# Attention steps in another order, the first unit chunk by chunk, and three sums moved in a hybrid decoder layer

## What is computed

```
x += 1/2 * SwiGLU_1(RMSNorm(x))                 # 1024 -> 2816 -> 1024
h  = RMSNorm(x);  p = h @ W_in
     gated linear attention: 4 heads, chunks of 64, a gate of rank 16
     dilated attention: 8 heads of 64, rotary on the first 16 of each head's dims
x += W_out @ concat(gla_out, attn_out)
x += 1/2 * SwiGLU_2(RMSNorm(x))
out = RMSNorm_final(x)
```

## Time and profile before

| | us |
|---|---|
| median of 3 runs (985.09 to 986.87) | 985.33 |
| the profiled execution's own time | 985.22 |
| its span in the trace | 983.4 |
| PE busy | 965.2 (98%) |
| DVE busy | 486.5 (49%) |
| ACT busy | 347.5 (35%) |
| POOL busy | 50.6 (5%) |

### The profile page before, as it was taken

One profiled execution on the slowest core, in us unless ns is written; L12 is line 12 of the kernel. 1 busy time (PEld: TensorE's weight loads), 2 busy tenths in 40 slices (PEclk: granted clock), 3 DMA queues, 4 the chain that ended last, 5 costly groups with the idle time before them and its releaser, 6 DMA issues.

```text
span 983.4 us, 11835 instructions
## 1 busy us (share of the span) xinstructions
PE 965.2 (98%) x4554; PEld 786.2 (80%) x4554; DVE 486.5 (49%) x616; ACT 347.5 (35%) x453; POOL 50.6 (5%) x35
## 2 busy tenths in 40 slices
PE   8999999999999999999989899999999999999997
PEld 6888888888888886888867678788888888888885
DVE  6854532244444456634386659644453234444325
ACT  7323221122232336331656764533322123322313
POOL 0850000000000000000021000000000000000000
PEclk9999999999999999999999999999999999999999
DMA  8232222323211233222121103223212232223212
GB/s 316 86 129 85 75 97 96 117 86 112 102 69 65 96 112 122 86 94 86 43 76 54 44 1 129 86 91 123 85 64 97 96 129 86 85 91 143 86 43 85
DMA packets 16305, 92.63 MB, mean 94 GB/s; under 512 B 1936, under 2 KB 2320, under 8 KB 8080
## 3 DMA queue, kind: packets, MB, share of 16 engines
q1 hardware_dynamic: 15984, 91.89, 26.4%
q10 hardware_dynamic: 288, 0.28, 0.1%
HBM read 90.07 MB, written 2.10 MB: 94 GB/s over the span
## 4 chain that ended last, share of the span: by engine, by line
PE 92%; DVE 3%; ACT 2%; issue 2%; DMA 1%; POOL 0%; SPq 0%; DVEq 0%; ACTq 0%; POOLq 0%
PE bank L1156 29%; PE bank L1157 28%; PE bank L1158 28%; PE bank L1467 1%; PE bank L1451 1%; PE bank L1437 1%; ACT w_hi L432 1%; DMA x<-in_xT 1%; DVE gt L963 0%; PE bank L1229 0%; PE bank L1359 0%; PE bank L1231 0%; PE bank L1236 0%; PE bank L1181 0%; PE bank L1410 0%
## 5 line engine op out<-in xcount | busy, mean ns | idle before, releaser
L1156 PE MATMUL bank<-h_hi,w_hi 128*128 128x512 f32 x824 | 323.8, 393 | 0.0
L1158 PE MATMUL bank<-h_hi,w_lo 128*128 128x512 f32 x824 | 320.7, 389 | 0.0
L1157 PE MATMUL bank<-h_lo,w_hi 128*128 128x512 f32 x824 | 320.7, 389 | 0.0
L432 ACT ACTIVATE w_hi<-raw 128x2048 fp32r<-128x2048 f32 (+2 forms) x88 | 156.6, 1779 | 338.2 <-PE bank L1158 336.7
L711 DVE TENSOR_TENSOR w_lo<-raw,w_hi 128x2048 fp32r<-128x2048 f32 (+2 forms) x88 | 187.0, 2125 | 85.2 <-ACT w_hi L432 85.0
L1156 PEld LDWEIGHTS bank<-h_hi,w_hi 128*128 128x128 f32 x824 | 154.7, 188 | 34.7 <-issue 2.1
L1157 PEld LDWEIGHTS bank<-h_lo,w_hi 128*128 128x128 f32 x824 | 154.7, 188 | 32.4 <-issue 1.0
L1158 PEld LDWEIGHTS bank<-h_hi,w_lo 128*128 128x128 f32 x824 | 154.7, 188 | 32.3
L757 DVE TENSOR_TENSOR prod<-bank,rstd 128x512 f32<-128x512 f32 x44 | 30.4, 690 | 183.6 <-PE bank L1158 183.6
L1156 PE MATMUL bank<-g_hi,w_hi 128*128 128x512 f32 x272 | 105.8, 389 | 0.0
L1157 PE MATMUL bank<-g_lo,w_hi 128*128 128x512 f32 x272 | 105.8, 389 | 0.0
(11 more groups left out here) (218 smaller groups left out, 858.8 us busy)
## 6 DMA issues: line engine op xcount, KB each, us to landing
raw<-in_up SPq DMA_DIRECT2D x43, 1024.0 KB, 4.8
raw<-in_w_proj SPq DMA_DIRECT2D x8, 1024.0 KB, 4.8
raw<-in_down1a SPq DMA_DIRECT2D x8, 768.0 KB, 4.3
raw<-in_down2a SPq DMA_DIRECT2D x8, 768.0 KB, 4.4
raw<-in_down1b SPq DMA_DIRECT2D x8, 640.0 KB, 3.8
raw<-in_down2b SPq DMA_DIRECT2D x5, 1024.0 KB, 4.8
raw<-in_w_v SPq DMA_DIRECT2D x4, 1024.0 KB, 4.8
raw<-in_w_o SPq DMA_DIRECT2D x4, 1024.0 KB, 4.8
```

The costliest lines, as they stand in the source:

```text
L432: nc.scalar.activation(w_hi[u % 2][:, 0:size], raw[u % 2][:, 0:size], ACT.Copy).then_inc(w_round, 1)
L1156: nc.tensor.matmul(out, a_hi, b_hi, start=first, stop=False)
L1157: nc.tensor.matmul(out, a_hi, b_lo, start=False, stop=False)
L1158: return nc.tensor.matmul(out, a_lo, b_hi, start=False, stop=last)
```

## The change

It has five parts.

1. **Start.** The first unit's weights go over ACT's DMA queue in four chunks, both tiles' columns together; SP loads `x` alone. PE makes both tiles of the unit chunk by chunk. ACT rounds unit 1 before it squares `x`.
2. **Channel sums.** In `second_unit` the channel sums stand behind tile 3, no longer before it; in the second FFN they stand behind the second tile of the first unit (`w == 1`).
3. **Gate weights.** Their scaling stands in the first FFN, before its first down phase.
4. **Attention.** Even steps divide both heads on DVE, odd steps both on ACT (from step 11: one each). DVE issues the rotation behind the scaling, `rotated` behind the concatenation; unit splits and head work move to other steps.
5. **The last split** of that loop, of unit U+14, is made in four quarters in steps 10 to 13 (ACT) and 11 to 14 (DVE).

```diff
@@ SP, phase
-                    for j, (lo, hi) in enumerate(FIRST_COLS):
-                        sp.dma_start(raw[0][:, lo:hi], source(0)[:, lo:hi]).then_inc(w_first[j], 16)
-                        sp.dma_start(x[:, j, :], xT_in[j]).then_inc(x_in[j], 16)
-                    for m in range(2, KC):
+                    for m in range(KC):
                         sp.dma_start(x[:, m, :], xT_in[m]).then_inc(x_in[m], 16)
-                    sp.dma_start(raw[0][:, D:UP_W], source(0)[:, D:UP_W]).then_inc(w_in[0], 16)
@@ ACT, start
+        FIRST_CHUNKS = ((0, 1), (1, 3), (3, 5), (5, KC))
+            for j, (_, hi) in enumerate(FIRST_CHUNKS):
+                landed = w_first[j] if hi < KC else w_in[0]
+                act.dma_start(first_part(raw[0][:], j), first_part(up1[0], j)).then_inc(landed, 16)
+                if j == 0:
+                    act.dma_start(gains[:].rearrange("p n a -> p (n a)"), gains_in).then_inc(gains_in_sem, 16)
             for m in range(KC):
...
+                for j, (lo, hi) in enumerate(FIRST_CHUNKS):
+                    if m == lo:
+                        act.wait_ge(w_first[j] if hi < KC else w_in[0], 16)
+                        nc.scalar.activation(first_part(w_hi[0][:], j), first_part(raw[0][:], j),
+                                             ACT.Copy).then_inc(first_round if hi < KC else w_round, 1)
-            for m in range(2):
-                square_first(m)
             split(1, 0, unit_size(1))
-            for m in range(2, KC):
+            for m in range(KC):
                 square_first(m)
@@ PE, first_unit, second_unit, up
+                                for w in range(2):
+                                    col = (w * KC + pos) * P
+                                    nc.tensor.matmul(ps[4 + w][:], w_hi[0][:, col:col + P], h_hi[:, pos, :],
+                                                     start=pos == 0, stop=False)
...
                         late_low(1, 0, 2, lambda: pe.wait_ge(w_round, 2), lambda: pe.wait_ge(w_split, 2))
+                        tile_of(1, 1, 3)
                         pe.wait_ge(const_landed, 32)
                         pe.wait_ge(first_sum, KC - 1)
                         channel_sums(0, 6, sumsq[:])
-                        tile_of(1, 1, 3)
...
-                            if first and w == 0 and layer:
+                            if first and w == 1 and layer:
@@ ACT, attention loop
+        SHARED_FROM = 11
+        def on_scalar(s, e):
+            return s % 2 == 1 if s < SHARED_FROM else e == 1
...
+            def round_quarter(u, q, tiles):
+                cols = slice(q * S, q * S + S)
...
-                if 1 <= k <= ATT_STEPS:
-                    scale_second(k - 1)
+                if 1 <= k <= ATT_STEPS and on_scalar(k - 1, 1):
+                    scale_scalar(k - 1)
                 if k >= 2:
                     move_probsT(k - 2)
-                if turn_of == 2 and n < 4:
+                if turn_of == 3 and n < 3:
                     split_next(U + 9 + n, 0, T + 19 + 2 * n)
+                if 10 <= k < 14:
+                    round_quarter(U + 14, k - 10, T + 25)
...
-                if turn_of == 3 and k >= 7:
-                    high_heads(k // 4 - 1)
+                if k in (9, 13, 15):
+                    high_heads((9, 13, 15).index(k))
@@ DVE, gate weights
+                    if layer == 0 and kind == "down" and a == 0:
+                        dve.wait_ge(ga_in, 16)
+                        nc.vector.tensor_tensor(w_gate[:], raw_ga[:],
...
@@ DVE, attention loop
-                if rotates:
-                    rotate(2 * n + turn_of // 2)
+                if k == 11:
+                    rotated(7)
                 if k:
                     scale_probs(k - 1)
                 if rotates:
-                    rotated(2 * n + turn_of // 2)
-                if turn_of == 2 and n < 4:
-                    split_next(U + 9 + n, 0)
+                    rotate(2 * n + turn_of // 2)
                 if k == 0:
                     gla_channel(3)
-                if 1 <= k <= 4:
-                    g = k - 1
+                if k in (1, 2, 4, 5):
+                    g = (1, 2, 4, 5).index(k)
                     low_concat(g, cat_lo[:, g, :], o_gla[g][:], cat_hi[:, g, :])
-                if turn_of == 3 and k >= 7:
-                    low_heads(k // 4 - 1)
-                if turn_of == 0 and k >= 12:
-                    add_heads(k // 4 - 2)
+                if rotates and k < 10:
+                    rotated(2 * n + turn_of // 2)
+                if turn_of == 3 and n < 3:
+                    split_next(U + 9 + n, 0)
+                if 11 <= k < 15:
+                    split_quarter(U + 14, k - 11)
+                if k in (9, 13, 15):
+                    low_heads((9, 13, 15).index(k))
+                if k in (14, 16):
+                    add_heads(k // 2 - 6)
```

More of the change, by code:

```diff
@@ L192, in layer_program @@
         const_landed = sem("const_landed")
-        w_first = [sem(f"w_first{j}") for j in range(2)]
+        w_first = [sem(f"w_first{j}") for j in range(3)]
         warm_zero = sem("warm_zero")
@@ L248, in layer_program @@
         ktail_out = sem("ktail_out")
-        probs_scaled = [sem(f"probs_scaled{e}") for e in range(2)]
+        dve_scaled = sem("dve_scaled")
+        act_scaled = sem("act_scaled")
         cat_round = sem("cat_round")
@@ L323, in head_tiles, with scaled_count @@
             return (o_hi[:, p, :], o_lo[:, p, :]) if p < 2 else (h_hi[:, 4 + p, :], h_lo[:, 4 + p, :])
+        def on_scalar(s, e):
+            return s % 2 == 1 if s < SHARED_FROM else e == 1
+        def scaled_count(s, e):
+            mine = on_scalar(s, e)
+            return sum(on_scalar(r, f) == mine for r in range(s + 1) for f in range(2) if (r, f) <= (s, e))
         def unit_size(u):
@@ L607, in exp_scores, with scale_scalar @@
                                          accum_out=den[:, q:q + 1]).then_inc(exp_done, 1)
[L609 to L612 removed]
+            def round_quarter(u, q, tiles):
+                cols = slice(q * S, q * S + S)
+                if q == 0:
+                    act.wait_ge(tile_done, tiles)
+                    act.wait_ge(w_in[u % 2], 16 * (u // 2 + 1))
+                nc.scalar.activation(w_hi[u % 2][:, cols], raw[u % 2][:, cols],
+                                     ACT.Copy).then_inc(quarter_round if q < 3 else w_round, 1)
+            def scale_scalar(s):
+                act.wait_ge(rden_done, s + 1)
+                for e in range(2):
+                    if on_scalar(s, e):
+                        strip = probs[s % PROB_BUFS][e][:, 0:P * (s % 4 + 1)]
+                        nc.scalar.activation(strip, strip, ACT.Copy,
+                                             scale=rden[:, 2 * s + e:2 * s + e + 1]).then_inc(act_scaled, 1)
             def move_probsT(s):
@@ L896, in scale_probs @@
                 dve.wait_ge(rden_done, s + 1)
-                strip = probs[s % PROB_BUFS][0][:, 0:P * (s % 4 + 1)]
-                nc.vector.tensor_scalar(strip, strip, rden[:, 2 * s:2 * s + 1], None,
-                                        ALU.mult).then_inc(probs_scaled[0], 1)
+                for e in range(2):
+                    if not on_scalar(s, e):
+                        strip = probs[s % PROB_BUFS][e][:, 0:P * (s % 4 + 1)]
+                        nc.vector.tensor_scalar(strip, strip, rden[:, 2 * s + e:2 * s + e + 1], None,
+                                                ALU.mult).then_inc(dve_scaled, 1)
             def low_heads(p):
@@ L1204, in first_unit, with part_ready @@
                     def first_unit():
+                        def part_ready(k, own, whole):
+                            j = first_part_of(k)
+                            if FIRST_CHUNKS[j][1] < KC:
+                                pe.wait_ge(own, j + 1)
+                            else:
+                                pe.wait_ge(whole, 1)
                         for pos in range(KC + 1):
                             if pos < KC:
-                                pe.wait_ge(first_round, min(pos // 2 + 1, 2))
+                                part_ready(pos, first_round, w_round)
@@ L1220, in first_unit @@
-                        last.then_inc(tile_done, 1)
-                        pe.wait_ge(tile_out, BANK_CREDIT)
-                        late_low(0, 1, 5, lambda: pe.wait_ge(w_round, 1), lambda: pe.wait_ge(w_split, 1))
+                                for w in range(2):
+                                    col = (w * KC + k) * P
+                                    nc.tensor.matmul(ps[4 + w][:], w_hi[0][:, col:col + P], h_lo[:, k, :],
+                                                     start=False, stop=False)
+                                    last = nc.tensor.matmul(ps[4 + w][:], w_lo[0][:, col:col + P], h_hi[:, k, :],
+                                                            start=False, stop=k == KC - 1)
+                                    if k == KC - 1:
```

(1 more changed line is left out.)

56 lines of the change are left out of this document (29 added, 27 removed).

## The result

| | before | after |
|---|---|---|
| median of 11 runs each, us | 985.31 (984.69 to 987.03) | 988.80 (985.64 to 990.98) |
| ratio, 95% interval | | 1.0030 (1.0017 to 1.0043) |
| profiled execution, us | 985.22 | 990.02 |
| its span, us; mean granted clock | 983.4; 0.997 | 988.2; 0.992 |
| PE busy, us | 965.2 | 969.4 |

A forecast was written before the change was run, and what follows sets the result against it. PE, busy 98% of the span, bounds the kernel, so only its waits count. Terms +3.6 + 1.7 - 1.25 - 1.1 - 1.6 - 3.3 = -1.95 took 985.22 to 983.3 us, range 979.5 to 986.5.

The forecast's parts named there:

- Start: First unit's loads and products: 0.5 gained at the second chunk's wait, 0.4 from restarts, together 0.9 us faster.
- The chance of 12% for slower: Rival: ACT becomes attention's bound, waits return at scores(5), scores(9) and scores(15), +3.95, 989.2 us; chance 12%.
- a first unit that stalls between its chunks: Sign listed as showing the forecast wrong, at the kernel's start; no size given.
- The sums behind tile 3: First FFN: the later sums delay unit 3's split, a new PE wait of 4.5 us; unit 3 starts 3.6 later.
- Clock behind it: After the new wait at unit 3, the granted clock falls and costs 1.7 us, bounds 0 and 3.4.
- Gate weights: Before the gate product: PE's 1.48 us for one product of 0.23 shrinks, -1.25 us.
- the second FFN: Tile 1 fills 1.25 us idle before the sums; unit 2 starts at 634.5 instead of 635.61, -1.1 us.
- Attention: Steps 0 to 10 give -1.6 us and steps 11 to 15 give -3.3 us, together -4.9.
- Steps 0 to 10: Attention: the 1.64 wait in step 4 goes, 0.1 charged each in steps 3 and 7; -1.6 us.
- The wait of step 2: Attention: the 0.98 us wait stays, since DVE's norm and POOL's product do not overlap; gain 0.
- the tail: Attention steps 11 to 15: 5.0 us go, new waits of 1.5 at scores(15) and 0.25 at transposes; -3.3.
- some 0.7 of short gaps: Attention steps 11 to 15: short gaps following the 2.61 wait go, part of the 5.0 us counted there.

The follow-up runs named there:

- SP's loads held: Changed kernel, weights still on ACT's queue, but SP holds its loads of x from the fourth on until the weights' second chunk has landed: 985.40 us.
- all but the start: Kernel before with the attention, gate weight and second FFN changes; its start and first FFN's sums stay as they were: 979.00 us, ratio 0.9940.
- weights on SP's queue: Changed kernel with the first unit's four weight chunks issued on SP's queue, each just ahead of its first piece of x: 986.06 us.
- SP's queue and sums early: Changed kernel with the weight chunks on SP's queue and the first FFN's sums ahead of tile 3 again: 980.50 us.
- contiguous chunks: Changed kernel with each first-unit weight chunk loaded as one contiguous piece a row, not two half-size pieces, still on ACT's queue: 985.82 us.
- the changed kernel's second profile: The changed kernel measured once more, as it is, on the same chip as the run with the filled first wait: 988.53 us.
- gate weights and second sums alone: Kernel before with only the gate weights scaled earlier and the second FFN's sums behind tile 1: 983.25 us.

## Why the prediction was wrong

**Start: -0.9 forecast, +2.9 measured** (unit 3 at 7.4 later, of which the wait accounts for 4.5). This is the step that failed, by 3.8 us. I bounded the gain at the second chunk "nothing, and the whole 1.60", so left no loss, and took 0.5 "because the bytes ahead of that chunk are nearly the same as before". The chunk came at 10.38 for the 7.7 of that sum, 2.7 late, and 1.4 of clock followed. The other half of the term was right: by the runs without a fall it is 21.4 from the second chunk to the late sums, for 21.7 by my sum. The bytes ahead of the load did not tell when it lands: with two queues on full engines it was the share of its queue that counted, and none of the rows of before showed such a case; so the bound had to reach to the other side. I had read ACT's five issues and charged them nothing: ACT's first operation came at 5.30. That is not what cost the 1.4, as the run with SP's loads held shows (its chunk came 1.4 earlier with the same issues); it can be part of the 0.8 by which even there the chunk is behind the 8.19 of before. The chance of 12% for slower sat on attention, where nothing of the kind happened; "a first unit that stalls between its chunks" stood in the list of what would prove me wrong, without a price.

**The sums behind tile 3: right.** Wait 4.5 forecast and 4.38 measured, chain 15.1 and 15.2.

**Clock behind it: +1.7 forecast, +2.5 measured**, within its bounds (0 to 3.4). What was missed is that it is charged per wait: two more falls came, 1.5 us at the start (8 products from 10.38 to 13.69 took 3.3 us for 1.8) and 1.5 behind scores(15). I had charged the clock for one wait and nothing for the others.

**Gate weights: -1.25, and -1.1 for the second FFN: right.** 2.4 by the profile, 2.2 by the run. The chain of unit 2, called even within 0.1, was: PE starts that unit 0.16 behind its last product.

**Attention: -4.9 forecast, -2.7 measured, -4.2 without the fall.** Steps 0 to 10 gave -1.7 for -1.6. The wait of step 2 stayed (0.74 for 0.98), beside about 0.3 at scores(5) and at scores(9) where I had charged 0.1 each. The reason given for step 2 was right: the head norm's product now stands beside POOL's, and ends 0.54 behind it. Before, then the change:

```profile
501.73 0.68 DVE L963 TENSOR_TENSOR gt<-gt 128x512 f32<-128x512 f32 x1
...
508.42 1.78 DVE L1009 TENSOR_TENSOR gt<-gt 128x512 f32<-128x512 f32 x1
...
507.93 1.73 POOL L440 TENSOR_TENSOR projT<-projT,rope_c 128x512 f32<-128x512 f32 x1 [5.36 <-DVE square L899]
```

It takes 1.1 us longer, which is the 1.1 that adding the durations side by side would have promised (the rule of the Trainium skill, SBUF — State Buffer, "Who interferes with whom", on which that term was weighed, holds in the new order too). In the tail the wait at scores(15) is 1.42 for 1.5 forecast and the one behind it 0.39 for 0.25. Of the 2.2 that attention is short of, 1.5 is the clock. The other 0.7 is the term "some 0.7 of short gaps", which did not go: from scores(11) to the heads' product it is 33.25 - 2.61 - 1.7 = 28.9 before, less its wait and its clock, and 30.70 - 1.42 - 0.39 = 28.9 in the run with all but the start, less its waits.

In all: 3.8 (start) + 0.8 (clock behind unit 3) + 2.2 (attention, 1.5 of it clock) = 6.8 between the forecast of -1.95 and +4.8. The median is kinder to it than the profiled execution, whose clock, 0.992, is among the lowest of the eleven.

## What to carry to other kernels

A load moved to a second engine's queue got no bandwidth of its own here: with the DMA engines full, small strided pieces lost against another queue's long ones, and the loads that are needed first should stay in one queue in the order of need, or the others be held. An operation that starts a long chain (here 15 us from the sums to a split) can't be put behind PE work for the sake of a 1 us gap, unless the work left behind it covers the chain. Price every wait of PE over about 1.4 us with the clock that may fall behind it, 1.4 to 3 us here, and put that on both sides of the range.

## What the runs showed of the hardware

The fall of the clock is not given by the length of the wait. The same wait of 1.42 us at scores(15) stands in eleven of the profiles; the clock was granted low behind it in five (the changed kernel, weights on SP's queue, SP's queue and sums early, SP's loads held, contiguous chunks) and stayed at 1.00 in six, among them the changed kernel's second profile. At the start, waits of 1.05 to 1.87 had none, those of 2.35, 2.47, 2.62 and 3.08 had one of 1.4 to 2.8 us (by the distance from the second chunk to the sums against the 21.4 of the runs without), and the one of 2.49 with twelve more products behind it had none in its profile. All seven waits of 4.4 had one, of 1.5 to 3.0 us (by the distance from unit 3 to the gate product against the 331.9 without). The length of the low stretch differs too: 3 us in one execution and 6 in another of the same kernel, after waits of 3.08 and 2.47. In attention's old order the wait of 2.61 had one in both profiles that hold it. The 1.64 at scores(5) had none in the kernel before, and one in the run with the gate weights and second sums alone (0.69 from 514 to 516 us, 0.50 from 516 to 518): there attention, from its first scores to the heads' product, takes 86.85 us for 85.25. What decides it within these waits stays open. These 1.6 us are also the size by which the runs of the kernel before fall apart, though no profile of one of its longer runs shows the place: of its runs, those near 985.3 have a mean clock of 0.996 to 0.998 and those near 986.8 mostly 0.994 to 0.996.

And a queue's share of full DMA engines went with its packets: the same 384 KB landed after 9.5 to 12.1 us (six profiles) in pieces of 1.5 KB and after 7.7 (one profile) in pieces of 3 KB, beside the same competitor.
